# Three of the four down quarters of an MLP as seven block products with weight sums formed in HBM

## The reference

```
u = rms_norm(h, norm_mlp_g[l])
h = h + jnp.square(jax.nn.relu(u @ w_mlp1[l])) @ w_mlp2[l]
return rms_norm(h, final_norm_g)
```

## Time and profile before

| what | us |
|---|---|
| median of three timed runs (1350.03 to 1350.37) | 1350.33 |
| span of the profiled execution, first to last instruction | 1348.7 |
| PE busy in it | 1334.4 |
| DVE busy | 939.1 |
| ACT busy | 586.7 |
| POOL busy | 70.7 |

### The profile page before, as it was taken

The page is one execution under the profiler, slowest core; times in us unless marked ns, Lnnn a source line. Parts: engine busy times, 40 slices in busy tenths (PEclk is TensorE's granted clock), DMA queues, the critical chain, the costliest instruction groups (busy, mean ns, idle before and its releaser), DMA issues.

```text
span 1348.7 us, 17627 instructions
## 1 busy us (share of the span) xinstructions
PE 1334.4 (99%) x6397; PEld 1094.9 (81%) x6397; DVE 939.1 (70%) x1503; ACT 586.7 (43%) x990; POOL 70.7 (5%) x60
## 2 busy tenths in 40 slices
PE   7999999999999999999999999999999999999998
PEld 6787777788888888888888888888888888888886
DVE  7868888885576543355445563599889988995685
ACT  7535655564555432114333344734333433333234
POOL 1000000102002000000013300000000000000000
PEclk9999999999999999999999999999999999999999
DMA  5333333243323333323333342323233223323332
GB/s 164 94 93 79 73 74 89 63 141 97 107 80 107 95 93 110 93 76 112 94 93 93 94 121 83 97 78 93 73 98 95 82 76 89 87 74 109 98 106 94
DMA packets 224104, 127.02 MB, mean 94 GB/s; under 512 B 21234, under 2 KB 214851, under 8 KB 224034
## 3 DMA queue, kind: packets, MB, share of 16 engines
q1 hardware_dynamic: 222418, 123.47, 31.9%
q10 hardware_dynamic: 1616, 2.62, 0.6%
HBM read 123.98 MB, written 2.10 MB: 93 GB/s over the span
## 4 chain that ended last, share of the span: by engine, by line
PE 97%; DVE 2%; ACT 1%; issue 0%; ACTq 0%; DVEq 0%
PE lin L668 26%; PE lin L671 26%; PE lin L672 26%; PE ob L1095 1%; PE sc L760 1%; PE sc L1051 1%; PE sc L1054 1%; PE sc L1055 1%; PE tr L773 1%; PE ob L797 1%; PE sc L784 1%; PE tr L1054 1%; PE lin L1054 1%; PE tr L1055 1%; PE lin L1055 1%; PE tr L1051 1%
## 5 line engine op out<-in xcount | busy, mean ns | idle before, releaser
L1719 DVE TENSOR_TENSOR wl<-raw,wh 128x1024 fp32r<-128x1024 f32 (+2 forms) x235 | 287.2, 1230 | 62.1 <-ACT wh L1228 57.7
L1228 ACT ACTIVATE wh<-raw 128x1024 fp32r<-128x1024 f32 (+2 forms) x235 | 238.8, 1022 | 134.9 <-DMA raw<-in_w_mlp_dram 44.2
L668 PE MATMUL lin<-uh,wh 128*128 128x512 f32 x624 | 249.8, 400 | 0.5 <-DVE ul L1791 0.4
L672 PE MATMUL lin<-uh,wl 128*128 128x512 f32 x624 | 243.2, 390 | 0.0
L671 PE MATMUL lin<-ul,wh 128*128 128x512 f32 x624 | 243.1, 390 | 0.0
L668 PE MATMUL lin<-vh,wh 128*128 128x512 f32 x512 | 202.6, 396 | 0.2 <-DVE te L2369 0.2
L671 PE MATMUL lin<-vl,wh 128*128 128x512 f32 x512 | 199.6, 390 | 0.0
L672 PE MATMUL lin<-vh,wl 128*128 128x512 f32 x512 | 199.3, 389 | 0.0
L668 PEld LDWEIGHTS lin<-uh,wh 128*128 128x128 f32 x624 | 117.2, 188 | 27.8 <-issue 4.4
L671 PEld LDWEIGHTS lin<-ul,wh 128*128 128x128 f32 x624 | 117.3, 188 | 25.1 <-issue 2.2
L672 PEld LDWEIGHTS lin<-uh,wl 128*128 128x128 f32 x624 | 117.1, 188 | 24.7
(11 more groups left out here) (555 smaller groups left out, 2085.2 us busy)
## 6 DMA issues: line engine op xcount, KB each, us to landing
raw<-in_w_in_dram SPq DMA_DIRECT2D x100, 512.0 KB, 3.8
raw<-in_w_mlp_dram SPq DMA_DIRECT2D x64, 512.0 KB, 4.0
raw<-in_w_out_dram SPq DMA_DIRECT2D x16, 512.0 KB, 3.7
raw<-in_w_xkv_dram SPq DMA_DIRECT2D x8, 512.0 KB, 3.7
raw<-in_w_proj_b_dram SPq DMA_DIRECT2D x8, 512.0 KB, 3.8
raw<-in_w_proj_a_dram SPq DMA_DIRECT2D x8, 512.0 KB, 3.7
xtok<-in_x_dram ACTq DMA_DIRECT2D x4, 512.0 KB, 5.0
raw<-in_w_mla_out_dram SPq DMA_DIRECT2D x4, 512.0 KB, 3.5
```

The lines of the kernel that those rows point to most:

```text
L668: ins = pe.matmul(o, wh[:, slot, at], xh_, start=start, stop=False)
L672: return pe.matmul(o, wl[:, slot, at], xh_, start=False, stop=stop)
L1228: act.activation(wh[:, c.slot(4), 0:size], raw[:, c.slot(2), 0:size], ACT.Copy).then_inc(hi_made, 1)
L1719: dve.tensor_tensor(wl[:, c.slot(4), 0:size], raw[:, c.slot(2), 0:size], wh[:, c.slot(4), 0:size].bitcast(F32), ALU.subtract).then_inc(lo_ ...
```

## The change

The MLP is cut into four quarters of 1024 hidden features, `up0`, `down0` to `up3`, `down3`, 8 up jobs each. `down3` is 8 ordinary jobs of one chunk. `down0` to `down2` take another form (`seven`).

**Seven products.** In each, two neighbouring feature tiles (even, odd) by the two halves of the tokens form a 2 x 2 block matrix A, and the same two tiles of rows of `w_mlp2` by the two halves of the 1024 output columns a block matrix B. Of 2 x 2 blocks, the product needs 8 block products, or 7 of sums of blocks (Winograd's form). Here the activations are the stationary operand: each block product of a pair of tiles is 2 x 3 matmuls of 128x512 (`seven_part`), over four pairs 24, so 7 x 24 = 168 matmuls for a quarter and not 192. They add up in four pairs of PSUM banks (`PART_X`, `PART_Q`, `PART_P`, `PART_R`: all eight banks); three pairs are used twice. DVE adds each finished pair to accumulators in SBUF (`part`, 14 operations of 128x512 in a quarter). Behind the third quarter 16 such operations form the blocks of the result out of them (`combine`), PE turns these back from tokens to features by 32 transposes (`turn_acc`), 4 before the fifth tile of each of the last six jobs of `up3` and 4 + 4 in the first of `down3`, and DVE scales and adds each to `h` (`turned_added`).

**Sums of activations.** For each pair of tiles DVE makes four sums of 256 columns (`sums`, in `SF`), ACT rounds them by three copies, DVE writes the low parts by three operations (`sums_low`).

**Sums of weights.** POOL issues 15 transfers from HBM to HBM for each quarter (`sum_weights`), copies and accumulating ones, in six steps, each waiting for the one before; 8 of the 14 chunks of such a quarter are loaded from a scratch that holds one block as it is and the sums of two and of three, two from one with the sums of four, four from `w_mlp2` itself. SP waits for them before the quarter's first load. A chunk of `seven` holds 12 matmuls and not 24, `raw` has two more slots there (`raw2`, `raw3`), and a quarter has 14 chunks and not 8. `sum_weights(0)` stands between the squares of the convolution and those of `xattn`, the other two behind those of the MLP.

**Others.** The work on the mask table of the second block (DVE, POOL) moves from behind `down0` into `down3`; a few semaphores are merged into a running count of DVE's own steps.

```diff
-          ("w_out", 12, 12), ("xq", 4, 4), ("xv", 4, 0), ("xo", 4, 8), ("up0", 16, 16), ("down0", 16, 8), ("up1", 16, 16),
-          ("down1", 16, 8), ("values", 8, 0), ("av", 8, 0),
+          ("w_out", 12, 12), ("xq", 4, 4), ("xv", 4, 0), ("xo", 4, 8), ("up0", 8, 8), ("down0", 14, 0), ("up1", 8, 8),
+          ("down1", 14, 0), ("up2", 8, 8), ("down2", 14, 0), ("up3", 8, 8), ("down3", 8, 8), ("values", 8, 0), ("av", 8, 0),
...
+        RAW_SLOTS = (raw[:, 1, :], raw[:, 0, :], raw2[:], raw3[:])
+        PART_X, PART_Q, PART_P, PART_R = (sc[0], sc[1]), (sc[2], ob), (lin[0], lin[1]), (tr[0], tr[1])
+        SUM_X1, SUM_P, SUM_X2, SUM_R2 = ((acc[:, n, 0, :], acc[:, n, 1, :]) for n in range(4))
+        SUM_Q1, SUM_Q2, SUM_R1 = (acc5[:, 0, :], acc5[:, 1, :]), (nlog[:], bias[:]), (atok_flat, te[:])
+        ACC_BLOCKS = ((SUM_X1, SUM_R2), (SUM_Q2, SUM_Q1))
...
+                sp.wait_ge(weights_summed, SUM_STEPS[-1] * (q + 1))
+                for v in range(SEVEN_CHUNKS):
+                    if v < 2:
+                        sp.wait_ge(lo_made, c.static - 1 + v)
+                    elif v > 3:
+                        sp.wait_ge(lo_made, c.static + v - 3)
+                    elif q == 0:
+                        sp.wait_ge(lo_made, c.static)
+                    if v < 8:
+                        src = pairs_of[q, v // 2, v % 2]
+                    elif v in (10, 13):
+                        src = fours_of[q, v // 13]
+                    else:
+                        tile = 2 * (v - 8 - v // 10) + 1
+                        src = rows[tile * P:(tile + 1) * P, :]
+                    sp.dma_start(RAW_SLOTS[v % 4], src).then_inc(SLOT_LANDED[v % 4], 16)
             for name, first in (("values", 5 * D), ("av", D)):
                 c, _ = phase(name)
...
+            def sum_weights(u):
+                k = a["w_mlp2"][0][u * FFQ:(u + 1) * FFQ, :].rearrange("(k two p) c -> two k p c", two=2, p=P)
+                even, odd = k[0], k[1]
+                b11, b12, b21, b22 = even[:, :, 0:512], even[:, :, 512:1024], odd[:, :, 0:512], odd[:, :, 512:1024]
+                x, y = pairs_of[u, :, 0], pairs_of[u, :, 1]
+                t1, t2, t3 = x[:, :, 512:1024], y[:, :, 0:512], y[:, :, 512:1024]
+                before = SUM_STEPS[-1] * u
+                pool.dma_start(x[:, :, 0:512], b11).then_inc(weights_summed, 16)
+                pool.dma_start(t1, b11).then_inc(weights_summed, 16)
+                pool.dma_start(t3, b12).then_inc(weights_summed, 16)
+                pool.wait_ge(weights_summed, before + SUM_STEPS[0])
+                pool.dma_start(t1, b12, accum_op=ALU.add).then_inc(weights_summed, 16)
+                pool.dma_start(t3, b22, accum_op=ALU.add).then_inc(weights_summed, 16)
+                pool.wait_ge(weights_summed, before + SUM_STEPS[1])
+                pool.dma_start(t2, t1).then_inc(weights_summed, 16)
+                pool.wait_ge(weights_summed, before + SUM_STEPS[2])
+                pool.dma_start(t2, b22, accum_op=ALU.add).then_inc(weights_summed, 16)
+                pool.wait_ge(weights_summed, before + SUM_STEPS[3])
+                for g in range(2):
+                    for n in range(2):
+                        at = fours_of[u, g][:, 512 * n:512 * n + 512]
+                        pool.dma_start(at, t2[2 * g + n]).then_inc(weights_summed, 16)
+                pool.wait_ge(weights_summed, before + SUM_STEPS[4])
+                for g in range(2):
+                    for n in range(2):
+                        at = fours_of[u, g][:, 512 * n:512 * n + 512]
+                        pool.dma_start(at, b21[2 * g + n], accum_op=ALU.add).then_inc(weights_summed, 16)
+                pool.wait_ge(weights_summed, before + SUM_STEPS[5])
...
             add_squares("conv")
+            sum_weights(0)
             add_squares("xattn")
 
-            pool.wait_ge(xo_low, XH)
+            add_squares("mlp")
+            for u in range(1, SEVENS):
+                sum_weights(u)
+
...
+            def seven_part(banks, left, k, weights, slot, half, first, last, signal):
+                at = slice(512 * half, 512 * half + 512)
+                high, low_ = left
+                for r in range(2):
+                    tok = slice(k + r * P, k + (r + 1) * P)
+                    ins = pe.matmul(banks[r][:], high[:, tok], wh[:, slot, at], start=first, stop=False)
+                    if weights and r == 0:
+                        ins.then_inc(chunk_entered, 1)
+                    pe.matmul(banks[r][:], low_[:, tok], wh[:, slot, at], start=False, stop=False)
+                    ins = pe.matmul(banks[r][:], high[:, tok], wl[:, slot, at], start=False, stop=last)
+                    if signal:
+                        ins.then_inc(part_ready, 1)
...
+                    pe.wait_ge(f_low, 12 * u + 3 * kk + 3)
+                    pe.wait_ge(lo_made, (x + 1).v())
+                    if kk == 0:
+                        if u:
+                            taken(u - 1, 10)
+                    seven_part(PART_X, even, 0, True, x.slot(4), 0, kk == 0, last, last)
+                    if kk == 0:
+                        if u:
+                            taken(u - 1, 12)
+                    seven_part(PART_Q, even, 256, False, x.slot(4), 1, kk == 0, last, last)
+                    pe.wait_ge(lo_made, (y + 1).v())
+                    if kk == 0:
+                        evacuated(pe, j + -2)
+                        evacuated(pe, j + -1)
+                    seven_part(PART_P, s2, 0, True, y.slot(4), 0, kk == 0, last, last)
+                    if kk == 0:
+                        if u:
+                            taken(u - 1, 14)
+                        else:
+                            pe.wait_ge(std_made, NORM_NO["mlp"] + 1)
+                    seven_part(PART_R, s3, 0, False, y.slot(4), 1, kk == 0, last, last)
+                for g in range(2):
+                    for kk in (2 * g, 2 * g + 1):
+                        odd, s4 = (fh[:, 2 * kk + 1, :], fl[:, 2 * kk + 1, :]), (s4h[:, kk, :], s4l[:, kk, :])
+                        w = c + (8 + kk + g)
+                        pe.wait_ge(lo_made, (w + 1).v())
+                        if kk == 0:
+                            taken(u, 2)
+                        seven_part(PART_X, odd, 0, True, w.slot(4), 0, kk == 0, kk == 3, kk == 3)
+                        if kk == 0:
+                            taken(u, 4)
+                        seven_part(PART_Q, s4, 0, False, w.slot(4), 1, kk == 0, kk == 3, kk == 3)
...
+                    job(c + m, j + m, DT, uh, ul, before=tiles_of(u_low, U0["mlp"]) if q == 0 and m == 0 else None,
+                        between={4: lambda f=m - 2: turn_acc(f)} if q == SEVENS and m > 1 else {})
...
+                        act.wait_ge(s_made, 4 * q + kk + 1)
+                        act.activation(fh[:, m - 1, 256:512], SF[:, 0, :], ACT.Copy)
+                        act.activation(sh[:, kk, :, :], SF[:, 1:3, :], ACT.Copy)
+                        act.activation(s4h[:, kk, :], SF[:, 3, :], ACT.Copy).then_inc(s_high, 1)
+                    if q == 0 and m == 3:
...
+            def sums_low(q, kk):
+                dve.wait_ge(s_high, 4 * q + kk + 1)
+                dve.tensor_tensor(fl[:, 2 * kk, 256:512], SF[:, 0, :], fh[:, 2 * kk, 256:512].bitcast(F32), ALU.subtract)
+                dve.tensor_tensor(sl[:, kk, :, :], SF[:, 1:3, :], sh[:, kk, :, :].bitcast(F32), ALU.subtract)
+                dve.tensor_tensor(s4l[:, kk, :], SF[:, 3, :], s4h[:, kk, :].bitcast(F32), ALU.subtract).then_inc(f_low, 1)
+            def sums(q, kk):
+                even, odd = tc, td
+                step(dve.tensor_tensor(SF[:, 0, :], even[:, 256:512], odd[:, 256:512], ALU.subtract))
+                step(dve.tensor_tensor(SF[:, 1, :], SF[:, 0, :], even[:, 0:256], ALU.subtract))
+                dve.tensor_tensor(SF[:, 2, :], even[:, 0:256], even[:, 256:512], ALU.subtract)
+                dve.tensor_tensor(SF[:, 3, :], odd[:, 0:256], SF[:, 1, :], ALU.add).then_inc(s_made, 1)
+            def turned_added(f):
+                dve.wait_ge(part_ready, SEVEN_PARTS * SEVENS + f + 1)
+                if f:
+                    dve.wait_ge(h_added, f)
+                step(dve.tensor_tensor(rbc[:], tr[f % 2][:], mlp_scale, ALU.mult))
+                dve.tensor_tensor(h[:, f, :], rbc[:], h[:, f, :], ALU.add).then_inc(h_added, 1)
...
+                    if q == SEVENS and m == 0:
+                        dve.wait_ge(part_taken, base)
+                        combine(SUM_P, SUM_X1)
+                        combine(SUM_R2, SUM_R1)
+                    if q == SEVENS and m == 1:
+                        dve.wait_ge(part_taken, base + 4)
+                        combine(SUM_X1, SUM_X2)
...
+                    r_, whole, n = (ta, tb)[m % 2][:], (tc, td)[m % 2], 256 if q < SEVENS and m % 2 == 0 else S
+                    dve.tensor_tensor(whole[:], r_, r_, ALU.mult).then_inc(f_sq, 1)
+                    dve.wait_ge(f_sq, DT * q + m + 1)
```

(23 more changed lines are left out.)

343 lines of the change are left out of this document (208 added, 135 removed).

## The result

| | us |
|---|---|
| before, median (1350.03 to 1350.37) | 1350.32 |
| with the change, median of four runs (1457.80 to 1463.84) | 1461.61 |
| ratio, with its 95% interval | 1.0822, 1.0805 to 1.0838 |
| predicted | 1354, range 1345 to 1385 |
| span of the profiled execution, before and after | 1348.7, 1462.1 |

8% slower, 77 us above the upper end of the range. The page of the changed kernel, against the earlier trace rows: shares of the busy engines, the clock that TensorE was granted in 40 slices, and the chain that ended last.

The account below looks back on a forecast made before the run. PE's matmul issue was taken to bound the kernel. Changes of -16.3 + 3.6 (PE), + 7.9 (turns), + 3.9 (banks), + 3.5 (`up3`) and + 1.0 (loads) gave +3.6 us: 1354, range 1345 to 1385.

Parts of the forecast that it names:

- PE's work: PE in the MLP: 72 fewer matmuls save 16.3 us, 32 transposes add 3.6; PE alone 12.7 us less.
- From up to down: Turns into `seven`: PE waits for the third chunk, 4.2 us in the first, 1.85 in the other two; 7.9.
- The banks: `PART_X` reused at the ninth chunk of `seven`: PE waits 1.3 us for DVE's reads, three times; 3.9.
- `up3`: DVE lowers, squares and combines there: PE waits 2.2 at the third job, 0.8 and 0.5 later; 3.5 us.
- the prediction without its loads: The forecast of 1354 without its 1.0 us for late loads; 1353 by its terms.
- `down3`: Mask table operations there cost nothing: DVE has about 5.2 us of work per job of 5.44; otherwise about 1 us.
- The sums: One set of weight sums in HBM takes 56 us at 3.3 us a MB, with bounds 39 and 103.
- The upper bound, 103: Length in us of a set of weight sums if transfers of 4x128x512 ran on four engines alone.
- The loads: Weight chunk loads sharing DMA engines with the sums: 1 us of PE waits, bounds 0 to 6.
- the rival with the quarter of the engines: Four-row transfers use a quarter of the engines: 34 us late at `w_out`, loads slower, 1391 and up; chance 0.11.
- The wait in `w_out`: The first set, ahead of POOL's `xattn` add, is hidden up to 69 us; beyond, PE waits one for one.

Follow-up runs that it names:

- the kernel without sums: The changed kernel with POOL forming no weight sums and chunks loaded from `w_mlp2` as it is (output not the reference's): 1358.38 us, ratio 1.0060.
- the kernel with the third and fourth chunk ahead: Against the changed kernel: no weight sums, table moved out of `down3`, third and fourth chunk of `seven` before activation sums, PE's combine wait at the transposes: 1343.93 us.
- The sets of 69.7 and 70.6 us: Changed kernel with transfers reordered to 128x4x512 (69.7; kernel 1379.5 us), and with each 4x128x512 transfer issued as four of 128x512 (70.6; kernel 1378.45 us).

## Why the prediction was wrong

Three steps failed: the length of a set of weight sums, what the sums do to the loads beside them, and `down3`. The terms in their order; what is measured is read from the kernel without sums, where no other is named.

*PE's work*, -16.3 + 3.6 = -12.7: right to about 1.5 us. Where hardly a wait is left (the kernel with the third and fourth chunk ahead), the MLP up to `down3` is 10.2 us shorter, with 1.0 us of waits in it. By the distance of starts the 32 transposes cost 3.8 us there; some 1.3 us stay unassigned.

*From up to down*, 7.9: measured 3.2, 1.6 and 1.6 without sums, 6.4. In the right place, by the right chain, a fifth too large.

*The banks*, 3.9: wrong without sums, where `PART_X` is never waited for. The chain was put one chunk too late. It let ACT round the tenth chunk once PE is in the eighth, by the text's "two ahead"; in the trace without sums ACT does so once PE is in the seventh (PE's first matmul of it is at 483.73), so three ahead. ACT at the tenth chunk, DVE at the reads:

```profile
484.21 1.06 ACT L1389 ACTIVATE wh<-raw 128x1024 fp32r<-128x1024 f32 x1 [1.66 <-PE sc L1122]
...
486.45 1.88 DVE L2398 COPY acc<-sc 128x512 f32<-128x512 f32 x3
```

DVE has read both banks of `PART_X` by 487.7, and PE wants them at 489.17: 1.4 us to spare, which is the forecast wait of 1.3 less one chunk of 2.72. In the changed kernel the wait showed once, 3.0 us, in a quarter that had other delays.

*`up3`*, 3.5: measured 1.3, 0.6 and 0.4, at the three places named, 2.3 in all.

These three terms were 6.6 us too high together, and `down3`, next, 7.8 too low. That the prediction without its loads came within 5.4 us of the kernel without sums is so in good part luck.

*`down3`*, "cost nothing": this step failed. The prediction counted 5.2 us of DVE work to a job of 5.44 and took the table's operations at what they are beside an idle POOL. They ran beside POOL's adds, together 18.6 us and not 6.2; and with the table gone a ring with ACT was left, in which POOL's second add makes the lowering 2.34 us for 1.23. It cost 7.7 us. The trace of before holds both halves of it, and the prediction read neither. In order of time, DVE at the table and in `down1`, and POOL there:

```profile
595.85 0.42 DVE L2193 TENSOR_SCALAR rbc<-atok 128x512 int32<-128x512 int32 x1
```

```profile
696.92 3.45 DVE L1719 TENSOR_TENSOR wl<-raw,wh 128x1024 fp32r<-128x1024 f32 x2 [1.20 <-ACT wh L1228]
```

```profile
697.02 2.27 POOL L651 TENSOR_TENSOR kt<-kt,tb 128x512 f32<-128x512 f32 x1
```

A table operation of 0.42 us with POOL idle, and two lowerings in 3.45 us beside POOL, where the earlier trace rows have 2.35.

*The sums.* The step that failed first is the length of a set: 56 us by 3.3 us a MB, with all transfers on all engines. It was 116 to 127. Of this 46 us are the shape; with 128 rows outermost a set still took 69.7, 14 more than forecast, for which no run here gives the cause. The upper bound, 103, had the mechanism and nearly the time, step by step: 13.4 forecast for the lone 1 MB copy, 15.9 measured; 26.8 for the lone accumulation, 29.6 measured. As a rival it had 0.11. I left it there because no row showed such a transfer, while every row showed another shape; that is a reason for wide bounds, not for a low chance.

The Trainium skill, "DMA: Bandwidth & Descriptors", section "Why a DMA increments its semaphore by 16 and not by 1", has a rule by which the one order gets 4 engines and the other 16. The runs agree: shares of 0.28 and 1.08 with one transfer in flight, and 15.6 and 8.7 us to landing for the same 1 MB. Which of the engines carried what the trace doesn't tell.

*The loads*, 1.0 with bounds 0 to 6: this step failed too, and it is the larger error in us. Even the rival with the quarter of the engines had them as "slower" and put no number to it. Measured: 27 us before `up0` and some 56 in the MLP. The bound let a load grow to 6 or 7 us, as if it met average traffic. It shares some engines packet by packet with transfers that keep them busy for 30 us at a time, and it has landed only when its part on these has: 20.9 us for a load of 3.7. Two slots of `raw` cover 8.

*The wait in `w_out`*: hidden up to 69 us and one for one beyond, said the prediction. For the set of 115.8 that is 47; the wait cost 24, because late loads had put PE back by 27 already, and 47 less 27 is 20. The sets of 69.7 and 70.6 us cost PE nothing at that place, but PE was 7 to 8 us late there too, so they don't test the 69 closely. The chain was right, as far as the runs show.

## What to carry to other kernels

A transfer that the trace doesn't show yet has to be priced with its order of dimensions, and its price for others is how long it keeps busy the engines that their loads need as well, not its share of the bandwidth. Put the 128 rows outermost, and let few transfers be in flight beside a stream of loads with two slots of cover. When work is moved on DVE, look at what POOL does at the new place, and follow the ring with ACT and not only the sum of DVE's work.

## What the hardware showed unexpectedly

Transfers on few engines slow a load that passes over these, though the others have nothing to do (a share of 0.56 with two of them): one packet of the load for one of the transfers, 330 and 329 in 8 us, and 20.9 us to landing for 3.7.

DVE beside POOL: 128x1024 took 2.34 us for 1.23, and 128x512 operations 1.40 to 1.79 for 0.42 to 0.69; with POOL's adds cut to a column all were back. The Trainium skill, "SBUF — State Buffer", section "Who interferes with whom", has a DVE instruction with two inputs in SBUF contend with a GpSimd instruction that reads SBUF, and the runs agree. It has a `tensor_scalar` do the same in a mode that takes two ports; the table's operations with one input were slowed too, in which mode the trace doesn't tell.

A wait of PE can cost twice. Behind the wait of 3.2 us in `down0` the clock stayed at full in one profiled execution and was half for 6.8 us in another, with 12 matmuls at 0.43 us, 2.7 us more (columns as above, of the kernels without sums, table in its old and new place):

```profile
475.00:480.00 5.00, 5.00 (x24) 4.14 (x23) 2.35 (x3) 2.12 (x2) 0.00 (x0) 1.00 0.95 331
```

```profile
470.00:475.00 5.00, 2.83 (x7) 2.28 (x8) 5.00 (x6) 3.39 (x4) 0.00 (x0) 0.60 0.39 117
```

The kernels of the experiments without sums spread by 0.5 to 3.3 us from run to run, the one before by 0.4 to 1.5; what else makes the spread stays open.
